# Stages of a two-block transformer kernel joined into one block, with the second weight chunk's low parts on GpSimd at four stage ends

## The reference

```python
# first block, two layers; h_ctx only in layer 0
h = h + ga1 * (attention(modulate(rms_norm(h, g_mix), sh1, sc1)) @ wo)      # neighborhood, then sliding window
h = h + ga2 * (square(relu(modulate(rms_norm(h, g_mlp), sh2, sc2) @ w1)) @ w2)
# second block, two layers
p = rmsnorm(h, pre_g) @ w_in
y = concat(diff_attention(p) * silu(z_a), mlstm(p) * silu(z_b)) @ w_out     # layer 0
h = h + rmsnorm(y, post_g)
y = (gelu(u) * spatial_mix(rmsnorm(gelu(v), sg_norm_g)) * silu(z)) @ w_out  # layer 1
h = h + rmsnorm(y, post_g)
```

## Time and profile before

| what | us |
|---|---|
| median of 3 runs | 2736.09 |
| lowest and highest run | 2734.33, 2740.17 |
| the profiled execution: first to last instruction | 2732.2 |
| TensorE busy (matmul) | 2622.8 |
| VectorE, ScalarE, GpSimd busy | 1546.6, 1073.3, 875.4 |

### The profile page before, as it was taken

The page is one execution under the profiler, slowest core; times in us unless marked ns, Lnnn a source line. Parts: engine busy times, 40 slices in busy tenths (PEclk is TensorE's granted clock), DMA queues, the critical chain, the costliest instruction groups (busy, mean ns, idle before and its releaser), DMA issues. The chain is left out here.

```text
span 2732.2 us, 38254 instructions
## 1 busy us (share of the span) xinstructions
PE 2622.8 (96%) x14748; PEld 2130.9 (78%) x14748; DVE 1546.6 (57%) x2893; ACT 1073.3 (39%) x1864; POOL 875.4 (32%) x651
## 2 busy tenths in 40 slices
PE   6899999999999999999889999999999999999997
PEld 4777786788888888766668888787778888788886
DVE  4434344687777778556664444544556445516555
ACT  4454545422222222565542322344553434542222
POOL 1211121243333333021124444333334333444443
PEclk8999999999999999999999999999999999999999
DMA  6323333223332332110012222322212221222221
GB/s 244 116 79 97 107 99 115 85 96 108 106 107 107 108 108 70 57 47 32 32 47 96 104 92 92 96 66 74 78 47 102 71 85 62 94 93 93 93 93 62
DMA packets 69652, 243.02 MB, mean 89 GB/s; under 512 B 11780, under 2 KB 29700, under 8 KB 49288
## 3 DMA queue, kind: packets, MB, share of 16 engines
q1 hardware_dynamic: 69512, 241.15, 25.8%
HBM read 239.02 MB, written 2.10 MB: 88 GB/s over the span
## 5 line engine op out<-in xcount | busy, mean ns | idle before, releaser
L248 POOL TENSOR_TENSOR w_lo<-w_raw,w_hi 128x512 fp32r<-128x512 f32 x612 | 820.2, 1371 | 1736.7 <-ACT w_hi L241 602.9
L287 PE MATMUL bank<-u_hi,w_hi 128*128 128x512 f32 (+1 forms) x1952 | 731.8, 375 | 10.8 <-DVE u_lo L547 5.0
L289 PE MATMUL bank<-u_hi,w_lo 128*128 128x512 f32 (+1 forms) x1952 | 719.4, 369 | 0.0
L288 PE MATMUL bank<-u_lo,w_hi 128*128 128x512 f32 (+1 forms) x1952 | 718.7, 368 | 0.0
L287 PEld LDWEIGHTS bank<-u_hi,w_hi 128*128 128x128 f32 x1952 | 368.9, 189 | 80.9 <-issue 14.0
L288 PEld LDWEIGHTS bank<-u_lo,w_hi 128*128 128x128 f32 x1952 | 368.9, 189 | 62.2 <-issue 2.5
L289 PEld LDWEIGHTS bank<-u_hi,w_lo 128*128 128x128 f32 x1952 | 368.5, 189 | 62.3
L1052 DVE SCALAR_TENSOR_TENSOR resid<-bank,mod,resid 128x512 f32<-128x512 f32 (+1 forms) x384 | 242.0, 657 | 140.5 <-PE bank L289 136.1
L287 PE MATMUL bank<-hid_hi,w_hi 128*128 128x512 f32 (+1 forms) x768 | 275.5, 359 | 0.0
L289 PE MATMUL bank<-hid_hi,w_lo 128*128 128x512 f32 (+1 forms) x768 | 273.0, 355 | 0.0
L288 PE MATMUL bank<-hid_lo,w_hi 128*128 128x512 f32 (+1 forms) x768 | 272.1, 354 | 0.0
(11 more groups left out here) (410 smaller groups left out, 3888.6 us busy)
## 6 DMA issues: line engine op xcount, KB each, us to landing
w_raw<-stream SPq DMA_DIRECT2D x150, 1024.0 KB, 4.9
w_raw<-stream SPq DMA_DIRECT2D x56, 512.0 KB, 4.4
ada_ring<-stream SPq DMA_DIRECT2D x48, 512.0 KB, 4.7
bias<-bias SPq DMA_DIRECT2D x192, 64.0 KB, 2.3
ada_more<-stream SPq DMA_DIRECT2D x6, 1024.0 KB, 13.2
resid<-h SPq DMA_DIRECT2D x2, 1536.0 KB, 8.7
w_raw<-stream SPq DMA_DIRECT2D x8, 256.0 KB, 3.9
out<-resid SPq DMA_DIRECT2D x8, 256.0 KB, 2.0
```

Source lines behind the costliest of these rows:

```text
L248: ins = eng.tensor_tensor(m.wl[:, s, w], m.raw[:, s, w], m.wh[:, s, w].bitcast(F32), ALU.subtract)
L287: pe.matmul(out, lh, rh, start=start, stop=False)
L288: pe.matmul(out, lh, rl, start=False, stop=False)
L289: return pe.matmul(out, ll, rh, start=False, stop=stop)
```

## The change

One block is opened after `prologue` and all later stages write into it. What the closing of a block had ordered is now ordered by waits by name:

- `Apply.dve` waits for the root of the statistics before its first scale. SyncE waits for it at the start of `mlp_stage`, `swa_stage`, `diff_stage` and `odd_stage`.
- TensorE and SyncE of `swa_stage` and `diff_stage` wait for the low parts of the second chunk where they need them.
- `mlstm_stage`: SyncE waits for the last `y_lo` of `diff_stage`, ScalarE for its last projection, TensorE for the last but one and the last read of the two PSUM banks it takes over.
- At the ends of `na_stage`, both `mlp_stage`s and `swa_stage` the low parts of slot 1 go from VectorE to the end of GpSimd's list.
- The two idle matmuls at the head of four stages go to the end of the stage before, which then has four.
- In the first `mlp_stage` two small instructions on `gsc` move ahead of the last sixteen output tiles.

The core of the diff:

```diff
+        if self.before:
+            dve.wait_ge(*self.before.rooted())
         scale(0)
...
-        with nc.Block() as block:
+        with nullcontext(m.block) as block:
             @block.sync
             def _(sp):
+                sp.wait_ge(*before.rooted())
...
                 split_lo_loop(pool, m, 8, [CHUNK] * 4, last=True)
                 after.add(pool)
+                coming.low(pool, 1)
...
-                keep_busy(pe, m, m.lin[0][:, 0:LAT], 2)
                 up_first()
...
-                keep_busy(pe, m, m.lin[3][:, 0:LAT], 2)
+                keep_busy(pe, m, m.lin[3][:, 0:LAT], 4)
...
-                    own(dve, D)
-                    for l in (1, 4):
-                        n = KT * (2 + l // 4)
...
-                coming.low(dve, 1)
...
# na_stage and swa_stage
                 after.add(pool)
+                split_lo(pool, m, 1, 1)
...
-                split_lo(dve, m, 1, 1)
...
# swa_stage
+                sp.wait_ge(*before.rooted())
                 load(fills[2])
+                sp.wait_ge(*loaded.lo.at(2))
                 load(fills[3])
...
                 queries_first()
+                pe.wait_ge(*loaded.lo.at(2))
                 keys(0, 0)
...
# mlstm_stage
+                sp.wait_ge(*attended)
...
                 act.wait_ge(*loaded.landed(1))
+                act.wait_ge(*projected)
                 high(1)
...
+                pe.wait_ge(*loaded.lo.at(1))
+                pe.wait_ge(*added[0])
                 project_half("qk", 0, 0, ("q", 0))
+                pe.wait_ge(*added[1])
                 project_half("qk", 0, 1, ("k", 0))
...
             prologue(nc, m)
+            m.block = ctx.enter_context(nc.Block())
             stats = na_stage(nc, m)
```

More of the change, by code:

```diff
@@ L1 @@
-from contextlib import ExitStack
+from contextlib import ExitStack, nullcontext
 import numpy as np
@@ L793, in columns, with mlp_stage @@
         return ins
-def mlp_stage(nc, m, layer, tok, rstd, first, second):
+def mlp_stage(nc, m, layer, tok, before, first, second):
+    rstd = before.rstd
     A, D, E = m.A, m.D, m.E
@@ L804, in mlp_stage @@
         flat = relu[:, :, :, :].rearrange("p a t n -> p (a t n)")
-        norm = Apply(m, rstd, tok, lambda k, w: m.gsc[:, layer, 1, k, w:w + 1],
+        norm = Apply(m, before, rstd, tok, lambda k, w: m.gsc[:, layer, 1, k, w:w + 1],
                      lambda k, w: m.mod[:, layer, 3, k, w:w + 1],
@@ L1111, in _ @@
                         up("d", 1, i)
+                if ada:
+                    own(dve, D)
+                    for l in (1, 4):
+                        n = KT * (2 + l // 4)
+                        dve.scalar_tensor_tensor(out=m.gsc[:, 1, l // 4, :, :], in0=m.mod[:, 1, l, :, :], scalar=1.0,
+                                                 in1=col(m, "g_rms")[:, n:n + KT][:, :, None].broadcast_to([P, KT, 2]),
+                                                 op0=ALU.add, op1=ALU.mult)
                 down_("v", None)
@@ L2035, in key_loads, with swa_stage @@
     return out
-def swa_stage(nc, m, rstd_u):
+def swa_stage(nc, m, before, loaded):
     A, D, E = m.A, m.D, m.E
@@ L2053, in swa_stage @@
         stat = sb("stat", [P, 2, 16])
-        norm = Apply(m, rstd_u, TOK, lambda k, w: m.gsc[:, 1, 0, k, w:w + 1],
+        norm = Apply(m, before, before.rstd, TOK, lambda k, w: m.gsc[:, 1, 0, k, w:w + 1],
                      lambda k, w: m.mod[:, 1, 0, k, w:w + 1], [pt[:, n, :] for n in range(3)] + [e[:, n, 0:LAT] for n in range(2)])
@@ L2622, in add_y, with diff_stage @@
                       ALU.add).then_inc(*m.D.mark(f"e_{name}"))
-def diff_stage(nc, m, rstd_u):
+def diff_stage(nc, m, before, loaded):
     A, D, E = m.A, m.D, m.E
@@ L4317, in program @@
                    m.stream[at + 3 * h + 1].rearrange("p (k n) -> p k n", k=KT)[:, :, 0:P]) for h in range(2)]
-        stats = mlp_stage(nc, m, 1, LAT, stats.rstd, [(slice(0, CHUNK), m.stream[at])], values)
-        loaded = diff_stage(nc, m, stats.rstd)
-        post0, first_fills = mlstm_stage(nc, m, loaded)
+        stats, coming = mlp_stage(nc, m, 1, LAT, stats, [(slice(0, CHUNK), m.stream[at])], values)
+        loaded, *done = diff_stage(nc, m, stats, coming)
+        post0, first_fills = mlstm_stage(nc, m, loaded, *done)
         odd_stage(nc, m, post0, first_fills, out)
```

46 lines of the change are left out of this document (23 added, 23 removed).

## The result

The changed kernel takes 2747.22 us (median of 6 runs, 2745.09 to 2749.22), the kernel before 2738.32 (6 runs beside them, 2734.33 to 2740.17). The ratio is 1.0035, with a 95% interval of 1.0024 to 1.0045: slower, by more than the 0.2% that a measurement of this kernel can tell.

A forecast was written before the change was run, and what follows sets the result against it. TensorE, in flight 2622.8 of 2732.2 us, bounds the kernel, so late stage heads count. Turns +5.15 and the last two places -1.56 give +3.6; clock falls +3.9 make +7.5: span 2739.7, median 2743.5, range 2735 to 2748.

The forecast's parts named there:

- turns with two falls or more: Forecast case: VectorE and GpSimd alternate on SBUF and TensorE's clock halves at two or more starts; slower, chance 0.53.
- The meetings go: At six stage ends the next work no longer waits for all engines: 4.3 + 1.0 + 0.56 = 5.9 us back.
- The four: Stage ends na to mlp, mlp to swa, swa to mlp, mlp to diff: earlier first scales, taken alone 4.3 us back.
- The fifth: Stage end diff to mlstm: TensorE's wait between its matmuls goes, 1.0 us back.
- the sixth: Stage end mlstm to odd: VectorE starts 0.06 us behind the root instead of 0.62, 0.56 us back.
- Turns: At four stage ends GpSimd's low parts and VectorE's `Apply` alternate on SBUF: +5.15 us, including the 4.3 given back.
- the give-back: The 4.3 us that earlier first scales return at four stage ends, already included in the +5.15.
- Rival 2: VectorE does not lose its turns, GpSimd starting pieces only when the port is free: 2730 to 2733, chance 0.14.
- The clock: TensorE's longer idle times before the first `u_lo` halve its clock at three of four places, 1.3 us each: 3.9.
- rival 3: Engines stay together; nothing gained at diff to mlstm and mlstm to odd: +5.1 without falls, 2741, chance 0.07.
- The hidden costs: Low parts three to four us later, SyncE's loads up to 4 us later, two gsc instructions moved: nothing lost.

The follow-up runs named there:

- The version with the pieces around `Apply`: Changed kernel with all low parts on VectorE, at two starts two pieces before the first scale and two behind the last `u_lo`: 2731.89 us, 0.9981 of the kernel before.
- the join alone: Changed kernel with the four sets of low parts back at the end of VectorE's list: 2735.60 us, ratio 0.9997 to the kernel before.
- the smaller pieces: Changed kernel with the four moved low parts cut into eight pieces of 256 columns instead of four of 512: 2739.94 us, 1.0009 of the kernel before.
- the memset: Changed kernel with GpSimd writing zeros to w_lo of the four chunks instead of subtracting: 2731.87 us, ratio 0.998 to the kernel before.
- the copy: Changed kernel with GpSimd copying w_raw to w_lo of the four chunks instead of subtracting: 2733.12 us, ratio 0.9985 to the kernel before.
- the move alone: Kernel before, its seven blocks kept, with the four low parts moved to the end of GpSimd's list: 2753.58 us, ratio 1.0051 to the kernel before.

## Why the prediction was right

The forecast was 2743.5 us on a median of 2736.09, 1.0027, in a range of 2735 to 2748. The measured ratio is 1.0035, and 1.0027 lies within its interval. Direction and likeliest case (turns with two falls or more) were right, and so were the sizes of most terms:

- **The meetings go.** Right. The scales start 0.03 to 0.06 us behind the roots. The four were put at 4.3, and the run with hardly any low parts gave 4.43. The fifth was put at 1.0 and gave 1.00, the sixth 0.56 and 0.60. What the prediction did not ask was what the join would give at the four places with the low parts left on VectorE: only 1.8 us of the 4.3.
- **Turns.** Right in mechanism and size, +4.78 against +5.15 with the give-back, and place by place 0.97, 1.31, 1.01, 1.49 against 1.05, 1.4, 1.1, 1.6. Each was put about 0.1 too high. The walk by "0.55 behind GpSimd's end, 1.15 behind VectorE's" held to a few hundredths: 0.54, and 1.12 from the end of the first scale (1407.57 + 1.75) to that of the low part (1410.44). Rival 2, in which VectorE keeps its turns, is excluded by the second scale and the first `u_lo`, which took 1.75 us each.
- **The clock.** Right in mechanism and number, three falls of four places, and 0.6 too small in size: 1.59, 1.34 and 1.59 us against 1.3 each, 4.5 in all. Keeping TensorE busy took the falls away and left the starts where they were. The one place that held was `na_stage` to `mlp_stage` with the shortest wait, 2.10 us. That it held was partly luck. The wait of 2.25 us that the prediction counted for a steady clock had half clock behind it in six of the ten traces (after among them). What the traces bear out is the long side: each of the sixteen waits of 2.7 us or more after the first 50 us of the ten traces was followed by half clock.
- **The new waits end where the meetings ended** (rival 3). Excluded by the fifth and sixth place.
- **The hidden costs.** Also right. The moved low parts are done at 1412.11 in after, and the first projection, which doesn't read them, takes TensorE some 11 us from 1412.81. SyncE did wait, as forecast: in after the load behind the low parts at `mlp_stage` to `swa_stage` goes out at 1096.32, when they end. TensorE lost nothing by it: with its clock held, the second `mlp_stage` takes the 352.53 us of before.

The terms of the sum were +7.5 and measured +7.7: 4.78 + 4.52 - 1.60. That they agree so well is in part luck, since the turns were put 0.4 too high and the falls 0.6 too low. The other 3.8 us between the two profiled executions are the attention of `swa_stage`, mostly half clock, and the wait for weights in `na_stage`. The medians lie 8.9 us apart, 1.2 more than the terms. The granted clock of the six executions of after is 0.986 to 0.988, and 0.990 on average over the 61 executions of before beside the experiments; an estimate from that is 16 us more at half clock, of which the three falls are 10. So some more half clock than the three falls is likely, but the runs are from different chips, and the interval takes in both 1.0027 and 1.0035. What starts such a stretch, and why it lasts 3.4 us in one run and 10.2 in the next, stays open. The version with the pieces around `Apply` has a long one at the same place and is still faster than before.

The Trainium skill, page "SBUF — State Buffer", section "Who interferes with whom", says who collides, and the runs agree in each part of it: a subtract and a copy on GpSimd, which read SBUF, make turns with VectorE's two-operand instructions, and a memset, which reads nothing, does not (0.75 us beside it). The same page, section "SBUF: two separate sides", says that the one that starts first has the shared ports "for the whole instruction". That is more than the rows have: the blocked scale ends 0.54 us behind the other's end, where 0.75 is its time alone. The trace of before also has the other side: `resid<-bank,mod,resid` of `mlp_stage` (L1052), which reads PSUM and one 128x512 operand from SBUF, takes 0.75 us on average both in the 118 cases with a low part of GpSimd beside it and in the 138 without.

## What to carry to other kernels

A meeting of all engines can be hidden in part behind work that one of them has left: with the low parts on VectorE, the join gave 1.8 us at the four places, and 4.4 with hardly any. Before taking a meeting away, see what the engine that comes next still has on its list. Moving work from VectorE to an idle GpSimd isn't free when both read SBUF and VectorE's instructions read two operands there: it can come back as turns on the very instructions that the path needs, and a wait grown by that can cost TensorE its clock as well. Where an engine waits anyway, its own idle time just ahead of the event, and behind the burst that follows, was the better place here.

## What was not expected of the hardware

A turn is not a whole instruction of the other: VectorE's 128x512 instruction blocked by GpSimd ended 0.54 us after GpSimd's end (0.75 alone), with subtracts and with copies alike. Why it needs less than its 0.75 us is not shown. An instruction of VectorE in turns took 1.75 us beside pieces of 128x512 and 1.21 beside 128x256, where 0.75 and 1.25 or 0.73 would add up to 2.0 and 1.5. Neighbours on one engine overlap a little, so the fairer count is from start to start: a turn is 1.67 us, where 0.67 (two scales alone take 1.42) and 1.25 would be 1.92.

Two operands in SBUF are not the only case that collides. In before `e<-e,stat` (L1747, TENSOR_SCALAR), with one 128x512 operand, takes 0.48 us, and 1.28 us the five times that it stands beside a low part.

GpSimd's times alone: 128x512 memset about 0.5 us, copy 0.61, subtract 1.25. And the waits of TensorE with what its granted clock did behind them. Those of 2.73, 3.05, 3.07, 3.23 and 3.70 us were followed by 0.50, those of 1.34 and 1.50 (the join alone) and 2.10 (after) by 1.00. Between them the length of the wait doesn't decide: the one of 2.25 or 2.26 us in the attention of `swa_stage` was followed by 1.00 in before, with the smaller pieces, the memset and the copy, and by 0.50 in after and the other five runs. A wait of 2.34 us (the move alone) was followed by 1.00. Other stretches of half clock stand behind waits of 2.1 us or less, and behind the same waits other runs kept 1.00; their cause is not shown.
